# Mixer's last tile in a macaron decoder step: where its second RMS statistic and norm stand beside the output projection's first blocks

## Chip, cores and metric

The program runs on the 8 NeuronCores of one Trainium2 chip, one copy of it on each core, without any exchange between them. Each core takes one prompt sequence of 2048 tokens and 16 sample sequences of 8 tokens (128 rows), 2176 rows in all. The metric is the device time of the slowest of the eight cores, in microseconds (us); lower is better. The time before is 1310.12 us (median of 3 runs, 1309.73 to 1310.42).

## The reference, cut to what matters

```python
h = x + 0.5 * rmsnorm(swiglu(rmsnorm(x, ffn1_pre_g), ...), ffn1_post_g)
n = rmsnorm(h, mix_pre_g)
b_a, c_a, h_a, u, v = split(n @ w_in)               # 5 x 512 columns
y_a = b_a * causal_dwconv(c_a * h_a)                # group A, 512 wide
y_b = u * chunk_spatial_mix(rmsnorm(v), w_s, b_s)   # group B, 512 wide
y = concat(rmsnorm(y_a, out_g_a), rmsnorm(y_b, out_g_b)) @ w_out
h = h + rmsnorm(y, mix_post_g)
h = h + 0.5 * rmsnorm(swiglu(rmsnorm(h, ffn2_pre_g), ...), ffn2_post_g)
h = h + rmsnorm(sigmoid(h @ ple_w_gate) * (p @ ple_w_proj), ple_post_g)
```

D_MODEL is 1024, the SwiGLU's hidden width 2816. The statistic that the change moves is the mean square of y_b over its 512 channels, and the norm is the scaling of y_a and y_b by their roots and gains.

## The kernel before

**Passes.** The rows of a core are done in two passes. Pass one (`P.idx` 0) has nine blocks of 128 rows in three tiles of 384 columns (the last block holds the sample rows); pass two (`P.idx` 1) has eight blocks in two tiles of 512. In each pass the stages follow each other on TensorE (PE): gate and up projection of FFN 1, its down projection, the mixer (`mixer`), the mixer's output projection, gate and up of FFN 2, its down projection, and the layer embedding. No scheduler orders the work: every engine's queue has the instructions in the order in which the Python code issues them, and semaphore waits tie the engines together (`Eng.wait`).

**The mixer's end.** The mixer works tile by tile with channels on the partitions. Per tile and channel group, DVE multiplies U's projection into `mixo` (y_b), and ACT squares the product into one of six `sq` buffers (`square`). `stat` lets PE sum four such squares over the partitions by a matmul with a matrix of 1/512 (`ones`, L711); `rstd_bc` is Ln and Exp on ACT, from the PSUM bank into the half `zsc[par, 512:1024]`. `norm_apply` is eight instructions on DVE that write y_a (c < 4) and y_b (c >= 4), scaled, into `nT`, the left operand of the output projection. For all tiles but the last this is done while the next tile runs. For the last tile it is left to `tail`, which `mixer` returns and the next stage calls:

```python
        def tail(ev):
            norm_apply(nt - 1, norm_stat(nt - 1))
        return norm_ev, tail, vo_ev["ev"]
```

**The output projection.** `tok_stage` loops over the blocks. `proj_block` projects a block of 128 tokens into a pair of PSUM banks by 16 matmuls 128x128 by 128x512 (L559, the last block L548). `post_stat` has ACT square the pair with a sum (`rstd_of`), then Ln and Exp. `post_apply` has DVE multiply the pair by the gain into `zsc[zi]`, which frees the pair, and then add the scaled result into the residual `h`. With lag 3, `pre_fn` of the block before comes next: ACT squares `h` with a sum, DVE writes the pre-normed block into `nbr`, and SP's queue turns it by a DMA transpose into `nT` for FFN 2. Block b needs `norm_ev[b]`; only the blocks of the last tile (6 to 8 in pass one, 4 to 7 in pass two) wait for the tail's norm.

**PSUM.** There are eight banks, taken in rotation. `get_bank` takes the next one; `get_pair` rounds up to the next even one, so a single bank taken between two pairs makes the rotation skip a bank. A bank is taken only when it has been freed.

**What follows.** Gate and up of FFN 2 (`gu_stage`, `gu_unit`) go through units of a weight slot and a tile. A unit is two halves, and each half is 16 matmuls (eight for the gate, eight for the up projection) into the next two banks. In both passes three units of tile 0 come first, so the first half needs the turned blocks of tile 0 only (0 to 2 in pass one, 0 to 3 in pass two). The banks are given back by Silu on ACT and a product on DVE, which stand in their queues behind the post norms of the last blocks.

Of the kernel before, what the change touches and what calls it, by code (L numbers as in the profile page):

```python
# [6 lines left out]
BF16 = mybir.dt.bfloat16  # L7
# [5 lines left out]
D = 1024  # L13
# [13 lines left out]
G1POST, GMPRE, GMPOST, G2PRE, G2POST, GPLE = range(6)  # L27
# [26 lines left out]
class Eng:  # L54
# [7 lines left out]
    def wait(self, *evs):  # L62
        best = {}
        for ev in _flat(evs, []):
            if ev.key not in best or best[ev.key].val < ev.val:
                best[ev.key] = ev
        for ev in best.values():
            if self.seen.get(ev.key, 0) >= ev.val:
                continue
            self.e.wait_ge(ev.sem, ev.val)  # L70
            self.seen[ev.key] = ev.val
            if _COLLECT is not None and ev.idx is not None:
                _COLLECT.add((ev.key, ev.idx))
# [47 lines left out]
def build_program():  # L121
# [38 lines left out]
    sg_t = nc.alloc_sbuf_tensor("sg", [128, 2, 512], F32)  # L160
# [17 lines left out]
    def nb(b, j0):  # L178
        return hmid[:, j0:j0 + 8, b * 128:(b + 1) * 128]
# [37 lines left out]
    def act(wait, **kw):  # L217
        ACT.wait(wait)
        return ACT.mark(nc.scalar.activation(**kw))  # L219

    def stt(wait, out, in0, scalar, in1, op0=ALU.mult, op1=ALU.mult):
        DVE.wait(wait)
        return DVE.mark(nc.vector.scalar_tensor_tensor(out=out, in0=in0, scalar=scalar, in1=in1, op0=op0, op1=op1))  # L223

    def tt(wait, out, in0, in1, op):
        DVE.wait(wait)
        return DVE.mark(nc.vector.tensor_tensor(out=out, in0=in0, in1=in1, op=op))  # L227
# [31 lines left out]
    def hold_fills(n=0):  # L259
        wr["limit"] = wr["issued"] + n  # L260
# [12 lines left out]
    def next_fill():  # L273
        f = wr["used"]
        wr["used"] += 1
        return f, fill_ev[f]
# [15 lines left out]
    def gain(i):  # L292
        return gain_t[:, i % 3, :]
# [4 lines left out]
    def rstd_of(src, junk, wait, n, c=1.0, stop=False):  # L298
        e = st_n["i"] % 16
        st_n["i"] += 1  # L300
        s = st_t[:, e, :]
        e1 = act(wait, out=junk, in_=src, func=AF.Square, accum_out=s[:, 0:1])
        if stop:
            return s, e1, n, c
        return rstd_rest((s, e1, n, c))

    def rstd_rest(a):
        s, e1, n, c = a
        e2 = act([e1], out=s[:, 1:2], in_=s[:, 0:1], func=AF.Ln, bias=c * EPS, scale=c / n)
        e3 = act([e2], out=s[:, 2:3], in_=s[:, 1:2], func=AF.Exp, scale=-0.5)  # L310
        return s[:, 2:3], e3, e1
# [6 lines left out]
    def turn_buffer():  # L318
        i = t_n["i"] % 2
        return nbr_t[:, i, :, :], t_ev[i]  # L320
# [10 lines left out]
    def pre(b, gi, dst, junk_wait=None):  # L331
        r, e3, _ = rstd_of(h_t[:, b, :], dst, [h_ev[b], junk_wait], D)
        e = stt([e3, gain_ev[gi]], dst, h_t[:, b, :].rearrange("p (k s) -> p k s", k=8), r,
                gain(gi).rearrange("p (k s) -> p k s", k=8))
        return e
# [187 lines left out]

    def post_stat(b, pair, ev, c, j0):
        pt, lo, hi = pair
        return rstd_of(pt[:].rearrange("p (k s) -> p k s", k=8), nb(b, j0), [ev], D, c)

    def post_apply(b, pair, st, gi):
        pt, lo, hi = pair
        zi = b % 2  # L530
        r, e3, e1 = st
        e = tt([e1, gain_ev[gi], zfree[zi]], zsc_t[:, zi, :], pt[:], gain(gi), ALU.mult)
        lo.free = hi.free = e
        h_ev[b] = zfree[zi] = stt([e, e3, h_ev[b]], h_t[:, b, :], zsc_t[:, zi, :], r, h_t[:, b, :], ALU.mult, ALU.add)
        return e
# [23 lines left out]
                ins = nc.tensor.matmul(o.t, lhs(k), sv, start=(k == 0), stop=(k == nk - 1))  # L559
        return pair, PE.mark(ins)  # L560

    def tok_stage(P, nk, nfl, lhs, wait, gpost, c, lag, j0, pre_fn, hooks=None):
        fl = [next_fill() for _ in range(nfl)]
        pend = None
        for b in range(P.nb):
            last = b == P.nb - 1
            pair, ev = proj_block(P, b, nk, lambda k, b=b: lhs(b, k), 4, fl, wait(b), last)
            if hooks and b in hooks:
                hooks[b](ev)
            st = post_stat(b, pair, ev, c, j0)  # L570
            e = post_apply(b, pair, st, gpost)
            if lag == 1:
                pre_fn(b, ev)
            else:
                if pend is not None:
                    pre_fn(*pend)
                pend = (b, ev)
        return pend
# [477 lines left out]
    for P in PASSES:  # L1056
        base = P.idx * NGAIN
        N = PASSES[P.idx + 1] if P.idx == 0 else None

        def guard1(j, P=P):  # L1060
            if P.idx == 0:
                return None
            lo, hi = j * 576 // 1024, (j * 576 + 575) // 1024
            evs = []
            for x in range(lo, hi + 1):
                if x < 4:
                    evs.append(out_ev[x])
                elif x < 8:
                    evs.append(xn_ev[1, 1][-1])
                else:  # L1070
                    evs += [xn_ev[1, 0][-1], out_ev[x - 2] if x < 11 else None]
            return evs

        def guard_none(j):
            return None

        if P.idx == 0:
            gu_stage(P, 3, guard1, {(1, 1): (1, start_square), (2, 0): (1, start_mid), (3, 0): (0, start_loads),
                                    (8, 0): (0, late_consts)},
                     [(0, 0), (0, 1), (1, 0), (1, 1), (2, 0), (2, 1), (0, 2), (1, 2), (2, 2)])  # L1080
        else:
            gu_stage(P, 3, guard1, {(0, 0): (1, next_square), (1, 0): (1, next_mid)})
        xn_ev.clear()
        def pre_mid(gi):
            def f(b, ev_d):
                dst, ev_t = turn_buffer()
                last_pre["ev"] = e = pre(b, gi, dst, [ev_d, ev_t])
                turn(b, dst, e)
            return f

        last_pre = {"ev": None}
        nT_ev.clear()
        hold_fills()
        tok_stage(P, NFF, 6, lambda b, k: hmid[:, k, b * 128:(b + 1) * 128], lambda b, P=P: [hm[P.tile_of(b)]],
                  base + G1POST, 4.0, 1, 14, pre_mid(base + GMPRE))
        pay_owed([nT_ev[P.nb - 1]])
        gain_load(base + G2PRE, [last_pre["ev"]])
        gain_load(base + G2POST, [last_pre["ev"]])

        norm_ev, tail, vo_last = mixer(P)  # L1100
        ACT.wait(vo_last)
        nT_ev.clear()
        pre_ffn2 = pre_mid(base + G2PRE)
        pend = tok_stage(P, 8, 2, lambda b, k: nT_t[:, k, b * 128:(b + 1) * 128], lambda b: [norm_ev[b]],
                         base + GMPOST, 1.0, 3, 0, pre_ffn2, {0: tail})
        ple_in = {}

        def last_norm(P=P):
            pre_ffn2(*pend)
            gain_load(base + GPLE, [last_pre["ev"]])  # L1110
            gain_load(base + NGAIN + G1POST, [last_pre["ev"]])
            POOL.wait(vo_last, last_pre["ev"])
            for i, r0 in enumerate(sorted(set([P.rows[0]] + ([P.rows[8]] if P.nb == 9 else [])))):
                n = 1024 if i == 0 else 128
                ple_in["ev"] = pt_sem.add(nc.gpsimd.dma_start(out=pT_v[:, :, i * 1024:i * 1024 + n],
                                                              in_=pT_d[:, :, r0:r0 + n]))
            pay_owed([nT_ev[P.nb - 1]])

        gu_stage(P, 3, guard_none, {(0, 0): (1, last_norm)})
        pT_ev = ple_in["ev"]  # L1120
        hold_fills(1)

        def next_x(ev):
            xt_load(PASSES[1], 0, 1, [ev])

        def cast(b, ev_d):
            dst, ev_t = turn_buffer()
            turn(b, dst, copy_v([h_ev[b], ev_t], dst, h_t[:, b, :].rearrange("p (k s) -> p k s", k=8)))

        nT_ev.clear()  # L1130
        tok_stage(P, NFF, 6, lambda b, k: hmid[:, k, b * 128:(b + 1) * 128], lambda b, P=P: [hm[P.tile_of(b)]],
                  base + G2POST, 4.0, 1, 0, cast, {8: next_x} if N is not None else None)
        guards["zsc"] = h_ev[P.nb - 1]
        groups = [[0, 1, 2], [3, 4, 5], [6, 7, 8]] if P.nb == 9 else [[0, 1], [2, 3], [4, 5], [6, 7]]
        ple(P, N, base, pT_ev, groups)
        if N is not None:
            pay_owed([xt_ev[1, 1]])
        zfree[0], zfree[1] = out_ev[4], out_ev[5]
# [101 lines left out]
```

How the kernel before makes its waits and increments, by code:

```python
    def wait(self, *evs):  # L62
        best = {}
        for ev in _flat(evs, []):
            if ev.key not in best or best[ev.key].val < ev.val:
                best[ev.key] = ev
        for ev in best.values():
            if self.seen.get(ev.key, 0) >= ev.val:
                continue
            self.e.wait_ge(ev.sem, ev.val)
            self.seen[ev.key] = ev.val
            if _COLLECT is not None and ev.idx is not None:
                _COLLECT.add((ev.key, ev.idx))
# [1 line left out]
    def mark(self, ins):  # L75
        self.idx += 1
        if _USED is not None and (self.name, self.idx) not in _USED:
            return Ev(self.sem, self.n, self.name, self.idx)
        self.n += 1
        ins.then_inc(self.sem, 1)
        return Ev(self.sem, self.n, self.name, self.idx)
# [8 lines left out]
    def add(self, ins):  # L90
        self.n += 16
        ins.then_inc(self.sem, 16)
        return Ev(self.sem, self.n, self.name)
```

## Time and profile before

| what | value |
|---|---|
| median of 3 runs | 1310.12 us (1309.73 to 1310.42) |
| the profiled execution | 1310.42 us |
| its span on the slowest core (core 6) | 1309.4 us |
| spans of the eight cores | 1305.4 to 1309.4 us |
| PE busy / DVE busy / ACT busy | 1282.9 / 523.4 / 418.6 us |
| chain that ended last, share of PE | 91% |

The span runs from the first to the last instruction of one core; the profiled execution's own time lies 1.0 us above it. Busy times of PE are of matmuls whose ends are modelled, so that a full PE shows as back-to-back rows. A row of the timeline gives start and duration, engine, line, operation, output and inputs, and in brackets how long the engine had been idle before it and what it then waited for; `x4` means that four instructions are merged in the row.

### The profile page before, as it was taken

The numbers are of one execution on the slowest core, as the hardware profiler recorded it, in microseconds if no ns is written. First come the engines' busy times: TensorE is split into PE (matmuls) and PEld (weight loads), VectorE is DVE, ScalarE is ACT, GpSimd is POOL, SyncE is SP. The second block draws the span as 40 slices with busy tenths as digits, with TensorE's granted clock in tenths as the row PEclk, the third lists the DMA queues.
The fourth block names the chain that finished last, engine by engine and source line by source line (L and its number), as shares of the span: only waits on it lengthen the run. The fifth ranks groups of instructions, "written<-read, shape, count | busy, mean of one in ns | idle before, by whom it ended". The sixth has DMA issues, their size and how long they took to land.

```text
span 1309.4 us, 18733 instructions; the slowest of 8 cores (1305.4 to 1309.4 us)
## 1 busy us (share of the span) xinstructions
PE 1282.9 (98%) x6734; PEld 651.5 (50%) x6816; DVE 523.4 (40%) x694; ACT 418.6 (32%) x870; POOL 94.6 (7%) x185
## 2 busy tenths in 40 slices
PE   8999999999999999999999999999999999999996
PEld 6566654455545666654444444444444444444442
DVE  3322223347697222222357321124467821212247
ACT  3311112344456111111168111123344811111137
POOL 2100000001001100000001100000010020000000
PEclk9999999999999999999999999999999999999998
DMA  9999322129625973231189996321396299333123
GB/s 214 173 213 216 66 49 49 29 42 179 117 48 90 178 130 65 49 65 33 28 176 257 219 200 113 62 49 25 76 170 117 57 159 171 65 66 56 33 41 129
DMA packets 88474, 139.89 MB, mean 107 GB/s; under 512 B 58304, under 2 KB 58560, under 8 KB 87872
## 3 DMA queue, kind: packets, MB, share of 16 engines
q0 software_dynamic: 25296, 90.25, 41.5%
q1 hardware_dynamic: 63088, 48.43, 13.7%
q8 instruction: 57, 0.93, 0.3%
q14 instruction: 33, 0.27, 0.1%
HBM read 206.03 MB, written 9.51 MB: 165 GB/s over the span
## 4 chain that ended last, share of the span: by engine, by line
PE 91%; ACT 3%; DVE 2%; issue 2%; DMA 2%; SPq 0%; ACTq 0%; DVEq 0%
PE ps L214 59%; PE ps L559 27%; PE ps L548 3%; DMA h<-xT 1%; PE ps L862 1%; ACT L219 1%; DVE big L223 1%; DVE big L227 1%; DVE nT L223 1%; PE ps L711 1%; ACT sg L219 1%; PE ps L502 0%; DMA nT<-nbr 0%; ACT big L219 0%; PE ps L807 0%
## 5 line engine op out<-in xcount | busy, mean ns | idle before, releaser
L214 PE MATMUL ps<-nT,ring 128*128 128x384 bf16 (+1 forms) x4127 | 768.7, 347 | 3.6 <-DMA nT<-nbr 1.1
L214 PEld LDWEIGHTS ps<-nT,ring 128*128 128x128 bf16 x4160 | 407.1, 98 | 361.1 <-issue 5.1
L227 DVE TENSOR_TENSOR big<-ps,sg 128x384 bf16<-128x384 f32 (+1 forms) x220 | 133.7, 610 | 464.7 <-PE ps L214 457.8
L559 PE MATMUL ps<-ring,big 128*128 128x512 bf16 x1291 | 283.7, 379 | 1.5
L219 ACT ACTIVATE sg<-ps 128x384 f32<-128x384 f32 (+1 forms) x237 | 126.5, 537 | 481.2 <-PE ps L214 477.5
L559 PEld LDWEIGHTS ps<-ring,big 128*128 128x128 bf16 x1320 | 129.2, 98 | 155.5
L255 POOL DMA_DIRECT2D ring<-w x170 | 90.2, 539 | 1043.6 <-PE ps L214 410.4
L219 ACT ACTIVATE big<-ps 128x1024 bf16<-128x1024 f32 (+4 forms) x89 | 75.3, 862 | 224.0 <-PE ps L559 192.9
L227 DVE TENSOR_TENSOR zsc<-ps,gains 128x1024 f32<-128x1024 f32 x51 | 62.3, 1222 | 180.6 <-ACT big L219 180.5
L559 PE MATMUL ps<-ring,nT 128*128 128x512 bf16 x470 | 104.7, 379 | 0.9 <-issue 0.4
L559 PEld LDWEIGHTS ps<-ring,nT 128*128 128x128 bf16 x480 | 46.8, 98 | 57.1 <-issue 1.3
L223 DVE SCALAR_TENSOR_TENSOR h<-zsc,st,h 128x1024 f32<-128x1024 f32 x51 | 65.5, 1285 | 11.1 <-DVE zsc L227 6.6
L227 DVE TENSOR_TENSOR big<-ps,big 128x384 f32<-128x384 f32 (+3 forms) x78 | 50.4, 679 | 37.3 <-PE ps L214 22.0
L223 DVE SCALAR_TENSOR_TENSOR nbr<-h,st,gains 128x1024 bf16<-128x1024 f32 x34 | 43.6, 1282 | 37.2 <-ACT st L219 37.2
L219 ACT ACTIVATE nbr<-h 128x1024 bf16<-128x1024 f32 x34 | 35.9, 1057 | 46.6 <-DVE h L223 42.0
L219 ACT ACTIVATE st<-st 128x1 f32<-128x1 f32 x205 | 41.7, 203 | 18.5 <-ACT st L219 0.5
L219 ACT ACT_TABLE_LOAD x31 | 39.8, 1283 | 10.8 <-PE ps L559 3.5
L219 ACT ACTIVATE big<-big 128x384 bf16<-128x384 f32 (+3 forms) x46 | 26.4, 605 | 38.7 <-DVE big L227 38.7
L548 PE MATMUL ps<-ring,big 128*128 128x512 bf16 x175 | 38.6, 379 | 0.1
L214 PE MATMUL ps<-ring,nT 128*128 128x512 bf16 x131 | 29.4, 379 | 0.3
L548 PEld LDWEIGHTS ps<-ring,big 128*128 128x128 bf16 x176 | 17.2, 98 | 20.8
L223 DVE SCALAR_TENSOR_TENSOR nT<-big,gc,zsc 128x384 bf16<-128x384 f32 (+1 forms) x40 | 23.9, 666 | 2.2 <-ACT zsc L219 2.2
(78 smaller groups left out, 366.4 us busy)
## 6 DMA issues: line engine op xcount, KB each, us to landing
ring<-w POOLq DMA_DIRECT2D x170, 512.0 KB, 15.0
h<-x SPq DMA_DIRECT2D x17, 512.0 KB, 36.9
gains<-gain SPq DMA_DIRECT2D x12, 512.0 KB, 11.2
y<-big SPq DMA_DIRECT2D x12, 512.0 KB, 11.5
big<-xT SPq DMA_DIRECT2D x2, 2048.0 KB, 14.5
h<-xT SPq DMA_DIRECT2D x2, 1536.0 KB, 13.1
y<-zsc SPq DMA_DIRECT2D x4, 512.0 KB, 6.7
h<-xT SPq DMA_DIRECT2D x2, 768.0 KB, 7.6
```

Of the source, the lines that this page charges most:

```text
L214: ins = nc.tensor.matmul(out_ap, l, r, start=(i == 0), stop=(i == n - 1))
L219: return ACT.mark(nc.scalar.activation(**kw))
L223: return DVE.mark(nc.vector.scalar_tensor_tensor(out=out, in0=in0, scalar=scalar, in1=in1, op0=op0, op1=op1))
L227: return DVE.mark(nc.vector.tensor_tensor(out=out, in0=in0, in1=in1, op=op))
L255: nc.gpsimd.dma_start(out=ring_t[:, s, o:o + HALF], in_=w_d[f % NFILL, :, o:o + HALF])))
L548: ins = nc.tensor.matmul(o.t, lhs(k), sv[:, k % per, half * 512:half * 512 + 512], start=(k == 0), stop=(k == nk - 1))
L559: ins = nc.tensor.matmul(o.t, lhs(k), sv, start=(k == 0), stop=(k == nk - 1))
L711: ins = nc.tensor.matmul(bank.t[:, 0:w], ones_t[:], sq[i][:, 0:w], start=(c == 0), stop=(c == 3))
L862: ins = nc.tensor.matmul(o.t, pT_v[:, k, b * 128:(b + 1) * 128], sv, start=(k == 0), stop=(k == 1))
```

## The change

Three things change. (1) In the mixer's output projection of pass one, `tail` is called behind the second block's projection and no longer behind the first one's: the hook goes from block 0 to block 1. (2) In pass two `tail` is called from a new place, `behind`, after block 0's `post_apply`. In both passes block 0's square, Ln, Exp, gain product and residual add now stand ahead of the tail's Ln, Exp and its eight norm instructions. (3) So that this is allowed, the junk output of the squares in `post_stat` goes into `sg` (first 1024 bf16 elements) and no longer into `big`, and the index of the scratch row `zsc` is passed in, so that block 0 takes the row that the tail doesn't use.

```diff
     def post_stat(b, pair, ev, c, j0):
         pt, lo, hi = pair
+        if j0 is None:
+            return rstd_of(pt[:], sg_t[:].rearrange("p a s -> p (a s)").bitcast(BF16)[:, 0:D], [ev], D, c)
         return rstd_of(pt[:].rearrange("p (k s) -> p k s", k=8), nb(b, j0), [ev], D, c)
 
-    def post_apply(b, pair, st, gi):
+    def post_apply(b, pair, st, gi, zi):
         pt, lo, hi = pair
-        zi = b % 2
...
-    def tok_stage(P, nk, nfl, lhs, wait, gpost, c, lag, j0, pre_fn, hooks=None):
+    def tok_stage(P, nk, nfl, lhs, wait, gpost, c, lag, j0, pre_fn, hooks=None, behind=None):
...
             if hooks and b in hooks:
                 hooks[b](ev)
             st = post_stat(b, pair, ev, c, j0)
-            e = post_apply(b, pair, st, gpost)
+            post_apply(b, pair, st, gpost, (b + P.idx + 1) % 2)
+            if behind and b in behind:
+                behind[b](ev)
...
         pend = tok_stage(P, 8, 2, lambda b, k: nT_t[:, k, b * 128:(b + 1) * 128], lambda b: [norm_ev[b]],
-                         base + GMPOST, 1.0, 3, 0, pre_ffn2, {0: tail})
+                         base + GMPOST, 1.0, 3, None, pre_ffn2,
+                         {1: tail} if N is not None else None, {0: tail} if N is None else None)
```

The order of PE's instructions at the output projection of pass one, before (`ps2` is the third of four bank pairs, `ones` the statistic's matrix):

```order
L214 MATMUL ps1<-nT,ring 128x384 x8
L559 MATMUL ps2<-ring,nT 128x512 x16
L711 MATMUL ps3<-big,ones 128x384 x4
L559 MATMUL ps0<-ring,nT 128x512 x16
L559 MATMUL ps1<-ring,nT 128x512 x16
L559 MATMUL ps2<-ring,nT 128x512 x16
L559 MATMUL ps3<-ring,nT 128x512 x16
```

And of the change, whose line numbers are three or one higher:

```order
L214 MATMUL ps1<-nT,ring 128x384 x8
L560 MATMUL ps2<-ring,nT 128x512 x16
L560 MATMUL ps3<-ring,nT 128x512 x16
L714 MATMUL ps0<-big,ones 128x384 x4
L560 MATMUL ps1<-ring,nT 128x512 x16
L560 MATMUL ps2<-ring,nT 128x512 x16
L560 MATMUL ps3<-ring,nT 128x512 x16
```

The statistic moves behind block 1, and block 1 moves from pair 0 to pair 3, the pair that block 4 takes. In pass two PE's order stays as it is.

DVE's queue at the same place of pass one, as one piece of difference (the lines around it are the last U products, which write `big`, and the eight norm instructions, which write `nT`):

```order
 L223 SCALAR_TENSOR_TENSOR nT<-big,gc,zsc 128x384 x8
 L227 TENSOR_TENSOR big<-ps,big 128x384 x4
+L227 TENSOR_TENSOR zsc<-ps,gains 128x1024
+L223 SCALAR_TENSOR_TENSOR h<-zsc,st,h 128x1024
 L223 SCALAR_TENSOR_TENSOR nT<-big,gc,zsc 128x384 x8
-L227 TENSOR_TENSOR zsc<-ps,gains 128x1024
-L223 SCALAR_TENSOR_TENSOR h<-zsc,st,h 128x1024
 L227 TENSOR_TENSOR zsc<-ps,gains 128x1024
 L223 SCALAR_TENSOR_TENSOR h<-zsc,st,h 128x1024
```

Block 0's two instructions now stand ahead of the tail's norm; the same two move in the same way in pass two. ACT's queue there, from the last three squares on, before in pass two:

```order
L219 ACTIVATE big<-big 128x512 x3
L219 ACTIVATE zsc<-ps 128x512
L219 ACTIVATE zsc<-zsc 128x512
L219 ACTIVATE big,st<-ps 128x8x128
L219 ACTIVATE st<-st 128x1 x2
L219 ACTIVATE big,st<-ps 128x8x128
```

And of the change:

```order
L219 ACTIVATE big<-big 128x512 x3
L219 ACTIVATE sg,st<-ps 128x1024
L219 ACTIVATE st<-st 128x1 x2
L219 ACTIVATE zsc<-ps 128x512
L219 ACTIVATE zsc<-zsc 128x512
L219 ACTIVATE sg,st<-ps 128x1024
```

Block 0's square and its two small steps now stand ahead of the tail's Ln and Exp (`zsc<-ps`, `zsc<-zsc`), in pass one too.

## Rows read from the trace of the kernel before

**Rows 1.** The page's fourth part: the chain that ended last, by engine.

```profile
PE 91%; ACT 3%; DVE 2%; issue 2%; DMA 2%; SPq 0%; ACTq 0%; DVEq 0%
```

**Rows 2.** Timeline of core 6, output projection of pass one (us start, us).

```profile
366.64 4.31 DVE L223 SCALAR_TENSOR_TENSOR nT<-big,gc,zsc 128x384 bf16<-128x384 f32 x8
...
370.87 1.94 DVE L227 TENSOR_TENSOR big<-ps,big 128x384 f32<-128x384 f32 x4
...
372.18 0.32 PE L711 MATMUL ps<-big,ones 128*128 128x384 bf16 x1
...
372.94 1.33 ACT L219 ACTIVATE big<-big 128x384 bf16<-128x384 f32 x3
373.13 2.21 DVE L223 SCALAR_TENSOR_TENSOR nT<-big,gc,zsc 128x384 bf16<-128x384 f32 x4 [0.32 <-ACT zsc L219]
...
373.58 1.15 PE L711 MATMUL ps<-big,ones 128*128 128x384 bf16 x3 [1.09 <-ACT big L219]
...
374.57 24.33 PE L559 MATMUL ps<-ring,nT 128*128 128x512 bf16 x110
...
376.04 2.21 DVE L223 SCALAR_TENSOR_TENSOR nT<-big,gc,zsc 128x384 bf16<-128x384 f32 x4 [0.70 <-ACT zsc L219]
...
384.74 1.22 DVE L227 TENSOR_TENSOR zsc<-ps,gains 128x1024 f32<-128x1024 f32 x1
```

**Rows 3.** Chain in order of time: an earlier statistic of four matmuls without a wait.

```profile
356.00 0.65 PE ps L711 x4
```

**Rows 4.** Timeline, FFN 1's down projection: square and gain product of block 0.

```profile
205.19 1.02 ACT L219 ACTIVATE big<-ps 128x1024 bf16<-128x1024 f32 x1 [10.25 <-PE ps L559]
...
206.48 1.23 DVE L227 TENSOR_TENSOR zsc<-ps,gains 128x1024 f32<-128x1024 f32 x1 [10.21 <-ACT big L219]
```

**Rows 5.** Timeline, pass one: last post norm and the start of FFN 2.

```profile
402.20 10.08 PE L214 MATMUL ps<-nT,ring 128*128 128x384 bf16 x61
...
407.46 1.22 DVE L227 TENSOR_TENSOR zsc<-ps,gains 128x1024 f32<-128x1024 f32 x1
...
410.06 0.87 ACT L219 ACTIVATE sg<-ps 128x384 f32<-128x384 f32 x2
...
411.25 1.02 DVE L227 TENSOR_TENSOR big<-ps,sg 128x384 bf16<-128x384 f32 x2
```

**Rows 6.** Timeline of core 6, output projection of pass two to the start of FFN 2.

```profile
998.84 5.38 DVE L223 SCALAR_TENSOR_TENSOR nT<-big,gc,zsc 128x512 bf16<-128x512 f32 x8
...
1004.14 2.48 DVE L227 TENSOR_TENSOR big<-ps,big 128x512 f32<-128x512 f32 x4
...
1006.66 1.65 ACT L219 ACTIVATE big<-big 128x512 bf16<-128x512 f32 x3
1006.85 2.74 DVE L223 SCALAR_TENSOR_TENSOR nT<-big,gc,zsc 128x512 bf16<-128x512 f32 x4 [0.24 <-ACT zsc L219]
...
1010.57 2.74 DVE L223 SCALAR_TENSOR_TENSOR nT<-big,gc,zsc 128x512 bf16<-128x512 f32 x4 [0.98 <-ACT zsc L219]
...
1013.23 1.22 DVE L227 TENSOR_TENSOR zsc<-ps,gains 128x1024 f32<-128x1024 f32 x1
...
1019.61 1.22 DVE L227 TENSOR_TENSOR zsc<-ps,gains 128x1024 f32<-128x1024 f32 x1
...
1029.78 1.28 DVE L223 SCALAR_TENSOR_TENSOR nbr<-h,st,gains 128x1024 bf16<-128x1024 f32 x1
...
1034.36 10.95 PE L214 MATMUL ps<-nT,ring 128*128 128x512 bf16 x49 [1.13 <-DMA nT<-nbr]
```

**Rows 7.** Windows, core 0: window, its us, PE busy (matmuls), granted clock, DMA share, GB/s.

```profile
318.00:330.00 12.00, 10.36 (x81) 1.00 1.04 155
```

**Rows 8.** The same window on core 6.

```profile
318.00:330.00 12.00, 10.42 (x72) 0.86 1.03 188
```

**Rows 9.** Waits of PE on core 6, 322 to 326 us: total, times, longest.

```profile
PE ps L807 <- DVE big L227: 1.6, 2, 1.0
```

**Rows 10.** Windows of core 6 at the program's end, columns as in group 7.

```profile
1297.00:1305.00 8.00, 0.29 (x2) 0.80 0.22 87
```

## The prediction

> **What bounds the kernel now.** I read the chain that ended last first: 91% of it is PE [rows 1], so a microsecond counts only if it lengthens or shortens a time in which PE stands. Then I read the timeline around both places that the diff touches, on PE for its gaps and on DVE and ACT for what ends them, and last the granted clock around gaps.
>
> In pass one PE stands in the middle of the statistic. It has the first of four matmuls at 372.18 and waits 1.09 us for ACT's squares before the second; block 1 starts at 374.57 [rows 2]. The same four matmuls take 0.65 us where nothing is waited for [rows 3], so the place costs 374.57 - 372.18 - 0.65 = 1.74 us of PE. In pass two the statistic has no such gap; there PE waits 1.13 us at 1034.36, for the turned block 3, before FFN 2 can start [rows 6].
>
> Behind both places DVE is the slower engine. The reader is to see in rows 2 and 6 that from the last U products on DVE has one instruction behind the other, with idle times of 0.32 and 0.70 us in pass one and 0.24 and 0.98 us in pass two, each for the Exp of a statistic. Blocks 2 to 8 of pass one begin their gain products between 384.74 and 407.46 [rows 2, 5], six steps of 3.79 us. PE needs (402.20 - 374.57) / 8 = 3.45 us for a block [rows 2, 5]. So PE runs ahead of DVE through this stage, and what matters at its end is when DVE is done, not when PE began.
>
> **What the change removes.** The 1.74 us stall of pass one. Block 1's matmuls (372.18 to 375.63) lie over the squares, which end at 372.94 + 1.33 = 374.27, and the statistic starts behind them without a wait. In pass two PE's order and its waits in the statistic stay as they are: nothing is removed there.
>
> **What it moves on DVE.** Before, DVE has something to do while ACT makes the statistics: the y_a half of the norm, at 373.13 and 1006.85. Now the next thing in its queue is block 0's gain product, and this waits for block 0's square, which on ACT stands behind the last three squares. From the start of such a square to the start of the gain product it is 206.48 - 205.19 = 1.29 us [rows 4]. Everything behind it in DVE's queue waits as well: residual add, the eight norm instructions, block 1.
>
> - Pass one: the square starts at 374.27, the gain product at 375.56. From block 0's gain product to block 2's it is 1019.61 - 1013.23 = 6.38 us, without the norm between them [rows 6]; these instructions are 128x1024 in both passes. The eight norm instructions take 4.31 us, or 370.87 - 366.64 = 4.23 us from start to start [rows 2]. Block 2's gain product starts at 375.56 + 6.38 + 4.27 = 386.21, against 384.74: DVE is 1.5 us late.
> - Pass two: the squares end at 1006.66 + 1.65 = 1008.31, the gain product starts at 1009.60. The eight norm instructions take 1004.14 - 998.84 = 5.30 us from start to start [rows 6]. Block 2 starts at 1009.60 + 6.38 + 5.30 = 1021.28, against 1019.61: DVE is 1.7 us late.
>
> **What the lateness costs PE.** In pass one it costs the gain of the stall. Block 1 now has bank pair 3, which block 4 takes. Block 4 could start at 372.18 + 3 x 3.45 + 0.65 = 383.18, and block 1's gain product ends at 375.56 + 2.6 + 4.3 + 1.2 = 383.7: PE waits 0.5 us. FFN 2 then starts at 402.20 - 1.74 + 0.5 = 401.0. Its first four half units take the pairs of blocks 5, 6, 7 and 8. A half is 16 matmuls at 10.08 / 62 = 0.163 us (one of 62 records is missing in the row of 61), 2.6 us. Before, the fourth starts at 402.20 + 7.8 = 410.0, and block 8's pair is free at 407.46 + 1.22 = 408.7 [rows 5]: 1.3 us to spare. Now PE is there at 408.8 and the pair is free at 410.2. PE waits 1.4 us and goes on at 410.2, 0.2 us later than before. The fifth half at 412.8 finds its bank free, since Silu there ends at 410.06 + 0.87 + 1.5 = 412.4, and the product by 411.25 + 1.02 + 1.5 = 413.8 frees the next banks in time. So pass one: -1.74 + 0.5 + 1.4, **+0.2 us**.
>
> In pass two PE already waits for block 3, and this wait is DVE's lateness and nothing else: `nbr` at 1029.78, PE at 1034.36, 4.6 us later [rows 6]. Everything before it moves by 1.7 us, with PE's own part unmoved, so PE's wait becomes 1.13 + 1.7 = 2.8 us: **+1.7 us**. The norm is done by 1012.1 + 5.3 = 1017.4, before block 4 wants it at 1008.89 + 3 x 3.45 = 1019.2 (1008.89 is 1034.36 - 1.3 - 7 x 3.45, with the array's gap taken as 1.3).
>
> The squares' new room costs nothing that I can see: instruction, engine and element count are the same, 1.02 us into `big` [rows 4]; `sg` is free, since its readers on DVE stand before the norm. A bound for it is 0.05 us a block either way, hidden under DVE's 3.79 us a block.
>
> **The clock.** The new 2.8 us wait of pass two may cost more than itself. At 322 to 325 us PE has two waits of together 1.6 us with short matmuls between them [rows 9]. Core 0 keeps a granted clock of 1.00 through 318 to 330 us (2.4 GHz), core 6 has 0.86 [rows 7, 8], that is a part at 1.2 GHz. Cores 1, 5 and 7 show what core 0 shows, cores 2, 3 and 4 what core 6 shows. A fall costs 12 x 0.14 = 1.7 us of PE. The other bound is the program's end: in 1297 to 1305 us PE is busy for 0.29 us, to about 1297.3, and the granted clock has a mean of 0.80 [rows 10], which is 8 x 0.2 / 0.5 = 3.2 us at 1.2 GHz. It fell at about 1301.8, after 4.5 us without a matmul. A wait of 2.8 us lies between the two; I take three in five for a core to fall, against four in eight at 322. The metric is the slowest of eight cores. Before, it held a core with one fall at 322, and on core 6 another at the start. Now most likely one core has both 322 and 1034, and this isn't sure to be the core with the longest rest. I take half of 1.7 us, **+0.9 us**, with 0 and 1.7 as its bounds.
>
> The Trainium skill (TensorE: Matmul & The Clock Gate, section Why this matters for your kernels) says that the array keeps its throughput through idle gaps shorter than a length which lies a little above the 2.8 us of this wait. By that rule the term is 0 and the time is that of rival 1; the trace doesn't agree at 322 us, where four cores fell with shorter waits.
>
> **The sum.** 0.2 + 1.7 + 0.9 = +2.8 us. The profiled execution took 1310.42 us with a span of 1309.4, and stands 0.3 above the median of the runs; the sum is a difference, so it goes on the median: 1310.12 + 2.8 = 1312.9 us.
>
> **Rivals.**
> 1. *The waits alone.* DVE is late as above and no core's clock falls more than before: 1310.1 + 1.9 = 1312.0. For it: the 4.5 us that the clock held at the end. Against it: the falls at 322 us. 26%.
> 2. *The lateness is absorbed in pass one.* The fourth half unit has 1.3 us to spare. If DVE is late by less than 1.3 - 1.2 = 0.1 us there, pass one gains; the 1.5 us would have to be wrong by most of it. With the full 1.74 gained and pass two at +1.7, the time stays at 1310.1. 8%.
> 3. *Faster.* The gain of 1.74 is kept and pass two isn't late, because ACT has block 0's square done before the three squares' results hold it, or block 0's early residual takes work off the end: 1308.4. It decides if block 0's gain product starts before 373.9 in pass one and 1007.9 in pass two. ACT's queue order speaks against it in both. 5%.
> 4. *Clock falls twice more.* The 1.4 us wait of pass one at 408.8, with 0.5 us some 25 us before it, brings a fall too, or one core has the full 1.7 and one at the start: 1310.1 + 1.9 + 3.4 = 1315.4. Against it: at 1034 us PE has waited 1.13 us without a fall. 11%.
>
> **How the numbers follow.** The forecast, late DVE and 0.9 (0.5 to 1.7) of clock, has 50%: 1312.5 to 1313.8. With rival 1 below it and part of rival 4 above it, the range is 1311.6 to 1314.8. A difference of 0.2% (2.6 us, here 1312.7) is about what a measurement of this kernel can tell from none. Slower by more than that: two thirds and more of the forecast's case and rival 4, 0.50. Within: the rest of it, rivals 1 and 2, 0.44. Faster by more: 0.06.
>
> **What would show it.** In the profile of the changed kernel: no wait of PE for squares in pass one's statistic; block 0's gain product about 2.7 us (pass one) and 3.0 us (pass two) behind the end of the U products, with DVE idle for that time; PE waits of some 0.5 and 1.4 us for DVE around 383 and 409; PE's wait for the turned block at FFN 2 of pass two at 2.8 us; a granted clock below 1.00 behind it on some cores. I would be wrong if DVE's steady 3.79 us a block weren't kept, or if block 0's gain product began much earlier.

## The result, and the profile after

The changed kernel takes 1314.63 us (median of 9 runs), the kernel before 1309.82 us (median of 9 runs beside them). The ratio is 1.0031 with a 95% interval of 1.0022 to 1.0041, or +4.1 us (2.9 to 5.4). The comparison leaves out runs in which a whole die was disturbed. Forecast were 1312.9 us, a difference of +2.8 us in a range of 1311.6 to 1314.8. The direction and the mechanism are as forecast. The size is 1.3 us more, which is just outside the interval of the difference, and the median lies only 0.2 us inside the top of the range.

The page's fourth part, to be held against [rows 1]: PE's share of the chain falls by three points; DVE's rises by two.

```profile
PE 88%; DVE 4%; ACT 3%; DMA 2%; issue 2%; SPq 0%; ACTq 0%; DVEq 0%
```

The timeline of core 0 after, at the output projection of pass one. The rows answer to [rows 2]; core 0's clock of the trace stands 1.4 us earlier than that of core 6 before, so distances are to be compared, not positions.

```profile
369.43 1.94 DVE L227 TENSOR_TENSOR big<-ps,big 128x384 f32<-128x384 f32 x4
...
371.50 1.33 ACT L219 ACTIVATE big<-big 128x384 bf16<-128x384 f32 x3
372.73 1.00 ACT L219 ACTIVATE sg<-ps 128x1024 bf16<-128x1024 f32 x1
...
374.07 1.22 DVE L227 TENSOR_TENSOR zsc<-ps,gains 128x1024 f32<-128x1024 f32 x1 [2.69 <-ACT sg L219]
374.19 0.81 PE L714 MATMUL ps<-big,ones 128*128 128x384 bf16 x4
...
376.66 4.32 DVE L223 SCALAR_TENSOR_TENSOR nT<-big,gc,zsc 128x384 bf16<-128x384 f32 x8
...
381.09 1.23 DVE L227 TENSOR_TENSOR zsc<-ps,gains 128x1024 f32<-128x1024 f32 x1
...
384.88 1.22 DVE L227 TENSOR_TENSOR zsc<-ps,gains 128x1024 f32<-128x1024 f32 x1
```

PE's four statistic matmuls stand together now and wait for nothing. DVE has an idle time of 2.69 us ahead of block 0's gain product, where it had 0.32 and 0.70 before the two halves of the norm. From the U products to block 2's gain product it is 384.88 - 369.43 = 15.45 us, before 384.74 - 370.87 = 13.87 us [rows 2]: DVE is 1.6 us late.

PE's rows of the same stage, up to the start of FFN 2. They answer to the PE rows of [rows 2, 5].

```profile
382.46 13.97 PE L560 MATMUL ps<-ring,nT 128*128 128x512 bf16 x64 [0.55 <-DVE zsc L227]
396.27 3.62 PE L549 MATMUL ps<-ring,nT 128*128 128x512 bf16 x16
399.72 5.36 PE L214 MATMUL ps<-nT,ring 128*128 128x384 bf16 x32
405.39 2.76 PE L214 MATMUL ps<-nT,ring 128*128 128x384 bf16 x16 [0.30 <-DVE zsc L227]
409.09 3.08 PE L214 MATMUL ps<-nT,ring 128*128 128x384 bf16 x18 [0.94 <-DVE zsc L227]
```

Three new waits, each for a gain product that gives back a pair of banks: for block 4, for the third half unit of FFN 2 and for the fourth. The fourth starts 409.09 - 369.43 = 39.7 us behind the U products, before 39.1 us (410.01 - 370.87 on core 6).

The start of FFN 2 in pass two on core 0, to be held against the last row of [rows 6]:

```profile
1028.69 3.62 PE L549 MATMUL ps<-ring,nT 128*128 128x512 bf16 x16
1035.37 9.94 PE L214 MATMUL ps<-nT,ring 128*128 128x512 bf16 x32 [3.06 <-DMA nT<-nbr]
```

The wait for the turned block 3 is 3.06 us where it was 1.13. The windows view from 1030 to 1042 us (window, its us, PE busy, granted clock, DMA share, GB/s), first core 0 and then core 6 of the changed kernel:

```profile
1030.00:1042.00 12.00, 8.94 (x29) 0.72 0.37 72
```

```profile
1030.00:1042.00 12.00, 8.94 (x42) 1.00 0.34 66
```

Both cores wait as long. Core 6 goes on at 2.4 GHz and has 42 matmuls in the window, core 0 goes on at 1.2 GHz and has 29. The granted clock was below 1.00 behind this wait on six of the eight cores (not on 3 and 6). Core 0 stood at 0.50 for 6.8 us in one piece, from 1034.4 to 1041.2:

```profile
1034.50:1041.10 6.60, 5.73 (x14) 0.50 0.24 46
1041.30:1042.30 1.00, 1.00 (x6) 1.00 1.06 205
```

Of this, 5.85 us lie behind PE's start at 1035.37 and cost it 2.9 us. Core 7 had the same 6.8 us, and these two are the slowest cores of the profile (1313.3 and 1313.4 us). The other four had 3.4 us at 0.50, which costs 1.7 us. Before the change the same window had 1.00 on all cores.

### The profile page after: what moved, and what is told of

Same layout as the page of the kernel before. It is cut to its first block, busy times and chain, and to the rows that moved or that the text cites. A ratio compares the mean times of both kernels' runs of the same rounds, so it can differ in the third digit from the quotient of the medians.

```text
span 1313.3 us, 18818 instructions; the slowest of 8 cores (1308.3 to 1313.4 us)
## 1 busy us (share of the span) xinstructions
PE 1289.9 (98%) x6816; PEld 652.1 (50%) x6816; DVE 523.5 (40%) x694; ACT 418.5 (32%) x870; POOL 94.3 (7%) x185
## 4 chain that ended last, share of the span: by engine, by line
PE 88%; DVE 4%; ACT 3%; DMA 2%; issue 2%; SPq 0%; ACTq 0%; DVEq 0%
PE ps L214 58%; PE ps L560 25%; PE ps L549 3%; DVE nT L223 1%; DMA nT<-nbr 1%; ACT sg L219 1%; DMA h<-xT 1%; PE ps L865 1%; DVE big L223 1%; DVE big L227 1%; ACT L219 1%; DVE nbr L223 1%; DVE zsc L227 0%; ACT big L219 0%; ACT nbr L219 0%
## 5 line engine op out<-in xcount | busy, mean ns | idle before, releaser
L219 ACT ACTIVATE sg<-ps 128x384 f32<-128x384 f32 (+2 forms) x254 | 143.7, 568 | 484.5 <-PE ps L214 479.4
L219 ACT ACTIVATE big<-ps 128x1024 bf16<-128x1024 f32 (+4 forms) x72 | 58.1, 827 | 223.0 <-PE ps L560 191.9
L223 DVE SCALAR_TENSOR_TENSOR big<-big,gc 128x384 f32<-128x384 f32 (+3 forms) x48 | 24.8, 590 | 0.0
```

## The experiments

Two theories were to be told apart, with variants. Mine: block 0's gain product now waits for a square behind ACT's last squares, DVE stands for it, and everything that DVE gives to PE afterwards is late; the longer wait in pass two then costs clock as well. The rivals: the squares' new room costs; pass one gains and only pass two loses; the wait alone costs and not the clock.

Since the slowest of eight cores moves by the falls of the clock, I give beside each ratio the mean span over the eight cores, averaged over the runs that the ratio compares, as a difference to the kernel before on the same chip. The number in brackets is a 95% interval from the spread of the variant's own runs; that of the kernel before adds about 0.2 us.

**room_only.** The squares' room and the scratch row as in the change, the tail where it was:

```diff
-                         {1: tail} if N is not None else None, {0: tail} if N is None else None)
+                         {0: tail})
```

> The squares' junk goes into sg and block 0 takes the other scratch row, but the tail is called where it was before, in both passes. If DVE's order is the cause (my theory), this is before within 0.5 us: PE stands 1.7 us in pass one's statistic and 1.1 us at FFN 2 of pass two. If the squares' new room costs (rival), ACT's squares are longer than 1.02 us and the time is 1 us or more above before.

Ratio 1.0000 (0.9991 to 1.0009), mean span +0.1 us (0.3). The groups by form show the square into `sg` at 1007 ns; into `big` it took 1019 ns in the profile before:

```profile
L219 ACT ACTIVATE sg<-ps 128x1024 bf16<-128x1024 f32 x17 | 17.1, 1007 | 1.3 <-PE ps L560 1.3
```

The room costs nothing. The rival falls.

**p1_only.** Pass one as in the change, pass two's tail as before:

```diff
-                         {1: tail} if N is not None else None, {0: tail} if N is None else None)
+                         {1: tail} if N is not None else {0: tail})
```

> Pass one as in the change (statistic behind block 1's projection), pass two's tail as before. My theory: PE's wait in the statistic is gone and comes back as waits for DVE's gain products, idle 0.55, 0.3 and 0.9 us, with PE 0.5 us later than before at the fourth half unit of FFN 2; time +0.5 us on before. Rival: pass one gains and all the loss is in pass two, then -1.7 us.

Ratio 1.0007 (0.9998 to 1.0016), mean span +0.7 us (0.3). PE's waits on core 1, 365 to 420 us (us in total, times, longest):

```profile
PE ps L214 <- DVE zsc L227: 1.2, 2, 1.0
PE ps L560 <- DVE zsc L227: 0.6, 1, 0.6
```

The wait for the squares is gone, and these stand in its place. That pass one gains 1.7 us is excluded; it loses about 0.5 (the stretches at the end of this section give 0.53).

**p2_only.** Pass one's tail as before, pass two's behind block 0's post norm:

```diff
-                         {1: tail} if N is not None else None, {0: tail} if N is None else None)
+                         {0: tail} if N is not None else None, {0: tail} if N is None else None)
```

> Pass one's tail as before, pass two's behind block 0's post norm. My theory: PE's wait for the turned block is 3.0 us instead of 1.1, and the granted clock falls behind it on five or more of eight cores; time +1.9 us by the wait and 1.7 to 2.8 us by the clock on the slowest core, +3.5 us together. Rival (the wait alone, no clock): +1.9 us. Rival (all loss in pass one): 0.

Ratio 1.0026 (1.0015 to 1.0036), +3.4 us; mean span +2.9 us (0.4). PE's waits on core 3:

```profile
PE ps L214 <- DMA nT<-nbr: 3.1, 1, 3.1
PE ps L714 <- ACT big L219: 1.1, 1, 1.1
```

The clock fell behind the wait on four cores of eight in the profiled execution. I had expected five or more. Most of the change's loss is here.

**late_dve.** The kernel before, with one more product on DVE and nothing moved:

```diff
     def post_apply(b, pair, st, gi):
         pt, lo, hi = pair
         zi = b % 2
         r, e3, e1 = st
+        if slow["on"] and b == 0:
+            zfree[zi] = tt([zfree[zi], h_ev[b]], zsc_t[:, zi, :], h_t[:, b, :], h_t[:, b, :], ALU.mult)
```

(`slow["on"]` holds in the mixer's output projection.)

> The kernel before with one more DVE product 128x1024 of 1.2 us ahead of block 0's gain product in both output projections of the mixer; its result is overwritten. If DVE's lateness is the cause, pass two's wait for the turned block grows from 1.1 to 2.3 us and pass one takes no new wait (it has 1.3 us to spare at the fourth half unit of FFN 2); time +1.2 us, and up to 1.7 us more where the clock falls behind the 2.3 us wait: +1.5 us. Rival (PE's own order decides, DVE has slack in both passes): 0.

Ratio 1.0024 (1.0015 to 1.0034), +3.1 us; mean span +2.5 us (0.3). Waits of PE on core 0 from 365 us on:

```profile
PE ps L214 <- DMA nT<-nbr: 2.3, 1, 2.3
PE ps L714 <- ACT big L219: 1.1, 1, 1.1
```

and its window:

```profile
1030.00:1042.00 12.00, 9.61 (x37) 0.86 0.34 66
```

DVE's 1.2 us come out as 1.2 us more wait in pass two. The view has no new wait in pass one, as expected, and yet FFN 2's fourth half unit starts 39.40 us behind the U products, where it was 39.13: DVE is 1.33 us late there (409.36 - 371.44 = 37.92 us to block 8's gain product, before 407.46 - 370.87 = 36.59), a little more than the 1.3 us to spare, and a stand of 0.27 us is hidden by the modelled ends. The time moved by twice what I had written. The clock fell behind the 2.3 us wait on four cores, which makes some 0.8 us of the mean. With 0.27 us in pass one and 1.33 us in pass two this is 2.4 us of the 2.5.

**split.** The change, with the tail's norm cut in two; `norm_apply` takes the channels, and the y_a half is called as soon as the mixer is done:

```diff
         def tail(ev):
-            norm_apply(nt - 1, norm_stat(nt - 1))
+            norm_apply(nt - 1, norm_stat(nt - 1), range(4, 8))
+
+        def first_half():
+            norm_apply(nt - 1, None, range(4))
...
+        first_half()
```

> The change, but the tail's norm is cut in two on DVE: the y_a half goes ahead of block 0's gain product, the y_b half behind block 0's residual add. My theory: the 2.7 and 3.0 us for which DVE stands before block 0's gain product are filled to below 0.5 us, DVE is 0.7 us (pass one) and 0.8 us (pass two) earlier than before, PE keeps the 1.7 us of pass one's stall and its wait in pass two falls to some 0.3 us: -2.5 us on before, -6 us or more on the change. Rival (block 0 ahead of the statistic on ACT is what costs, whatever DVE does meanwhile): no better than the change, +3 to +4 us.

Ratio 0.9988 (0.9979 to 0.9998), -1.6 us; mean span -2.2 us (0.2). DVE on core 2 in pass one:

```profile
372.36 1.94 DVE L227 TENSOR_TENSOR big<-ps,big 128x384 f32<-128x384 f32 x4
374.62 2.21 DVE L223 SCALAR_TENSOR_TENSOR nT<-big,gc,zsc 128x384 bf16<-128x384 f32 x4 [0.32 <-ACT zsc L219]
377.00 1.23 DVE L227 TENSOR_TENSOR zsc<-ps,gains 128x1024 f32<-128x1024 f32 x1 [0.17 <-DVE nT L223]
...
386.07 1.22 DVE L227 TENSOR_TENSOR zsc<-ps,gains 128x1024 f32<-128x1024 f32 x1
```

and its PE where FFN 2 begins, in pass one and in pass two:

```profile
410.27 1.95 PE L214 MATMUL ps<-nT,ring 128*128 128x384 bf16 x11 [0.37 <-DVE zsc L227]
...
1033.63 6.63 PE L214 MATMUL ps<-nT,ring 128*128 128x512 bf16 x30 [0.41 <-DMA nT<-nbr]
```

Block 0 still stands ahead of the statistic on ACT, and the statistic behind block 1 on PE; only DVE's hole is filled. The loss turns into a gain. DVE is 386.07 - 372.36 = 13.71 us from the U products to block 2, 0.16 us better than before and 1.74 us better than the change. I had expected 0.7; a wait of 0.47 us ahead of block 1's gain product, which I can't name, took part of it. PE keeps 1.5 us from pass one and 0.7 us from pass two (its wait there is 0.41 us where it was 1.13), together the 2.2 us of the mean span.

**fill_gap, fill_gap_again, change_again.** The change with 12 matmuls whose result nobody reads, where PE waits in pass two:

```diff
+    def keep_busy(n):
+        bank = banks[rot["n"] % 8]
+        PE.wait(bank.free)
+        for _ in range(n):
+            nc.tensor.matmul(bank.t, ones_t[:], wmT_t[:].rearrange("p h s -> p (h s)")[:, 0:512], start=True, stop=True)
+        bank.free = []
...
+        if N is None:
+            keep_busy(12)
         gu_stage(P, 3, guard_none, {(0, 0): (1, last_norm)})
```

> The change with 12 extra matmuls 128x128 by 128x512 (ones by mask weights, result overwritten) between the output projection and FFN 2 of pass two, where PE would stand for 3.1 us; they add no work behind the wait. Clock theory: PE's real work goes on at the same moment as in the change, but the granted clock stays at 1.00 behind it on all cores; the slowest core loses 1.7 to 2.8 us less, time -1.5 us on the change, +2.4 us on before. Rival (the clock costs nothing here, only the wait does): no change on the change, +4 us on before.

It gave 1.0026 (1.0016 to 1.0035), +3.4 us, against 1.0031 (1.0022 to 1.0041), +4.1 us, for the change on another chip: too near to tell. The mean span was +2.9 us (0.3). So I ran both on one chip.

> The change itself, on the same chip as the next run, to compare the two by all cores and not by the slowest alone. Clock theory and its rival: +3 to +4 us on before, with a granted clock below 1.00 at 1034 us on most cores.

> The change with the 12 extra matmuls in the wait of pass two, on the same chip as the run before. Clock theory: no fall at 1034 us on any core, a mean granted clock higher by 0.0007 (1.7 us at half speed on five to six of eight cores of 1310 us), a mean span 1 us below the change's. Rival (extra matmuls hold up the real work by as much as the clock gives): mean spans equal within 0.3 us.

The change: 1.0032 (1.0019 to 1.0045), mean span 1311.1 us (0.5) from four runs, +3.5 us on before, mean clock 0.9951. With the extra matmuls: 1.0010 (1.0000 to 1.0021), mean span 1309.4 us (0.3) from seven runs, +1.8 us, mean clock 0.9963. The timeline of the filled kernel on core 2 (the U products of DVE there start at 1003.82), and its window:

```profile
1029.29 3.62 PE L556 MATMUL ps<-ring,nT 128*128 128x512 bf16 x15
1032.74 2.75 PE L411 MATMUL ps<-wmT,ones 128*128 128x512 bf16 x12
1035.94 9.22 PE L214 MATMUL ps<-nT,ring 128*128 128x512 bf16 x41 [0.45 <-DMA nT<-nbr]
```

```profile
1030.00:1042.00 12.00, 11.50 (x54) 1.00 0.35 68
```

The change on the same core, same chip (U products at 1002.95):

```profile
1035.08 10.26 PE L214 MATMUL ps<-nT,ring 128*128 128x512 bf16 x39 [3.04 <-DMA nT<-nbr]
```

```profile
1030.00:1042.00 12.00, 8.91 (x34) 0.86 0.37 72
```

The real work goes on at the same moment in both, 1035.94 - 1003.82 = 32.12 us and 1035.08 - 1002.95 = 32.13 us behind the U products. The wait for data is the same; only PE's standing is gone, and with it the fall of the clock, on all eight cores in both profiles of the filled kernel (it fell on six and five of eight in those of the change). The mean span is 1.7 us (0.6) lower on this chip. So the clock's part is real; the slowest core's time differs by 2.9 us here (1.0032 against 1.0010), with wide intervals. The size is better read from the stretches below, since the same filled kernel was +2.9 us in mean span on one chip and +1.8 us on the other, which no profile explains.

**fill322 and split_fill.** 27 short matmuls in the two waits at 322 us of pass one, on the kernel before and on the split one:

```diff
+                    if P.idx == 0 and ti == 0 and c == 0 and i:
+                        for _ in range((0, 18, 9)[i]):
+                            nc.tensor.matmul(bank.t[:, 256:384], ones_t[:], wmT_t[:, 0, :], start=True, stop=True)
```

> The kernel before with 27 extra matmuls of 128 columns between the spatial matmuls of the first tile of pass one (at 322 to 325 us), where PE waits for DVE twice; their result is overwritten. Clock theory: the granted clock stays at 1.00 there on all cores, and the slowest core is 1 us (0 to 1.7) faster than before. Rival: the extra matmuls last longer than the waits, 0 to +0.5 us.

> The tail cut in two as in the split kernel, and the extra matmuls at 322 us. If the two gains add: split's -1.6 us and some -1 us, together -2.5 us on before. If the clock at 322 us costs nothing: split's -1.6 us.

fill322: 0.9996 (0.9987 to 1.0005), mean span -0.1 us (0.3). The window 318 to 330 us of core 6, to be held against [rows 8], has no fall any more, nor on any other core:

```profile
318.00:330.00 12.00, 12.00 (x110) 1.00 1.04 157
```

Yet the time is that of before, where I had expected 1 us less. The extra matmuls don't hold up the real ones: from the first spatial matmul near 322 us to the last tile's U products it is 46.6 us on all eight cores with them, and without them 46.6 us on a core whose clock holds and 48.3 us on one whose clock falls. In the ten other profiles, before's among them, the clock fell there on 23 of 80 cores, 0 to 5 of eight; at 1.7 us each that makes 0.5 us of the mean, which the spread can just hide. split_fill is the fastest: 0.9980 (0.9971 to 0.9990), -2.6 us, mean span -2.2 us (0.2). Whether its lead over split is real stays open, as the mean spans are equal.

**What each part costs, read from stretches.** The start of the last tile's U products on DVE is the same instruction in every kernel. The stretch from it in pass one to it in pass two holds pass one's part of a change and no fall of the clock. The stretch from there to the start of the program's last matmul holds pass two's part and the fall at 1034 us. The table has medians in us over the cores of the profiles; "held" are the cores whose clock held behind the wait, "fell" those with 3.4 us at 0.50, "fell long" those with 6.8 us.

| kernel | pass one to pass two | to the last matmul, held | fell | fell long |
|---|---|---|---|---|
| before | 633.27 | 292.77 | | |
| p1_only | 633.80 | 292.78 | | |
| p2_only | 633.29 | 294.70 | 296.38 | |
| the change, two profiles | 633.80 | 294.69 | 296.38 | 297.57 |
| the change with 12 matmuls, two profiles | 633.79 | 294.69 | | |
| late_dve | 633.54 | 294.10 | 295.72 | |
| split | 631.78 | 292.06 | | |

In the first stretch the cores of one kernel lie within 0.1 us of each other. In the second one a few cores have one more DMA wait at some 1054 us, which the medians leave out. So the change costs 0.53 us in pass one and 1.92 us in pass two, 2.45 us together, on every core. Behind the wait a short fall costs another 1.7 us and a long one 2.9 us. With the 12 matmuls the second stretch has the length of a core whose clock held, on nearly all of 16 cores, so they take the clock's price away and cost nothing themselves.

## Why the prediction was right, and where its size was off

**Bound.** PE and DVE's pace behind it, right: late_dve shows that 1.2 us more on DVE are 1.2 us more of PE's wait in pass two.

**Removed.** 1.74 us of stall in pass one, right; the wait for squares is in no profile with the statistic behind block 1.

**DVE's lateness.** Predicted 1.5 and 1.7 us, measured 1.6 (above) and, in pass two, 1.9: on core 0 from the U products at 1003.22 to block 2's gain product at 1020.61 it is 17.39 us, before 1019.61 - 1004.14 = 15.47 [rows 6]. The missing 0.2 us are in the step from the norm to block 1's gain product: eight instructions whose first starts at 1011.33 are followed by the gain product at 1016.81, 5.48 us and not 5.30.

**Pass one's price.** Predicted +0.2, measured +0.5 at the fourth half unit and in the stretch of the table, and +0.7 (0.3) as mean span of p1_only. Place and kind of the waits were right, but there are three and not two, and each costs more than its idle time shows. The idle times of 0.55, 0.30 and 0.94 us are counted from modelled ends, and a matmul's modelled end lies past the next one's usual start: 379 ns is the duration in the rows, 3.45 / 16 = 216 ns the spacing. So the array stands about 0.16 us longer each time.

**Pass two's price.** Predicted 2.8 us of wait and +1.7 us, measured 3.0 to 3.1 us on all cores and +1.9 us.

**The clock.** This is the term that was mis-sized most: +0.9 us predicted, with 1.7 as its bound. The two waits make 0.5 + 1.9 = 2.4 us, so 1.7 us of the measured 4.1 are left for it, with the interval of 1.2 us each way that the difference has. On the mean core of the change's profile it is (4 x 1.7 + 2 x 2.9) / 8 = 1.6 us. I had taken 1.7 us as the price of a fall from the one at 322 us and halved it for the slowest core. The price holds for a short fall (1.69 us in the table). What I hadn't reckoned with are two cores of eight with a fall of twice the length, 2.9 us, and these two were the slowest. My reason for the halving holds as far as it goes, since the slowest core had falls before the change too: one at the start and one at 322 us, 6.8 us at 0.50 together. The two slowest cores now have the one at 322 us and the long one, 3.4 + 5.85 = 9.3 us at 0.50 with work for PE. In this pair of profiles that is 1.2 us of PE's time more.

**Rivals.** Rival 1 (the waits alone, +1.9) is excluded by the clock behind 1034 us and by the table: the same waits cost 1.7 to 2.9 us more on a core whose clock fell. Rival 2 and the faster rival fall with p1_only and p2_only. Rival 4's 1315.4 us lies nearer to the measured 1314.63 than my 1312.9 does. Its first form didn't come: no profile of the changed kernel has a fall at pass one's new waits. Its second, the full price at 1034 us on a core that also fell at the start, is there (core 2 of the changed kernel, core 7 of change_again), but on the profile's slowest cores it was the long fall that made the time, and no rival had that. That the range held, by 0.2 us, is partly luck.

The Trainium skill's limit for idle gaps (TensorE: Matmul & The Clock Gate, section Why this matters for your kernels) lies above 2.3 us, and the trace doesn't agree: behind late_dve's 2.3 us wait the clock fell on four of eight cores. Behind 1.13 us it fell on none.

**Open.** Why the clock falls on one core and not on the next behind the same wait isn't shown. A fall at the start of the program, at 18 to 21 us, is in 30 of 96 cores of the profiles, in four of eight of fill322 and in one of eight before; it comes by chance, and a straight line fitted through the 96 core spans gives it the same 1.7 us as the others. The 0.47 us wait of split isn't explained.

## What to carry to other kernels

A stall taken from PE is worth something only if the engine that feeds PE next isn't made later by it: look for what the following engine did meanwhile, and leave it something to do. Here DVE's y_a half filled the time of the statistic, and moving it whole behind block 0 made DVE 1.6 to 1.9 us late, while cutting it at the point where its second input comes brought 1.6 us on the kernel before. A wait of 2.3 to 3.1 us on PE has a second price in clock on half of the cores or more, here 1.7 or 2.9 us. Matmuls without a use, put into the wait, avoided it on all 16 cores looked at and held up nothing. To price one part of a change, measure between two instructions that all kernels share: these stretches agree within 0.1 us, where the time of the slowest of eight cores moves by more than a microsecond from run to run.

## What the runs showed that was not expected

With waits of the same length the granted clock fell on some cores of a chip and not on others: behind 3.1 us on six, five and four of eight, behind 2.3 us on four, behind 1.13 us on none. The stretch at 0.50 had one of two lengths. It was 3.4 us where the fall came behind PE's start, and also on the five cores where it came 0.04 to 0.63 us ahead of it. It was 6.8 us on the three cores where it came 0.95 us or more ahead of it (cores 0 and 7 of the changed kernel, core 7 of change_again).
